# Hymba decode step on one core: mLSTM numerators issued head by head instead of in pairs of heads

## The reference

```python
    S = jnp.einsum('bhtd,bhsd->bhts', q, k) * D
    num = inter[..., None] * jnp.einsum('bhtd,bhde->bhte', q, C) + jnp.einsum('bhts,bhse->bhte', S, v)
    den = inter * jnp.einsum('bhtd,bhd->bht', q, n) + S.sum(axis=-1)
    h = num / jnp.maximum(jnp.abs(den), jnp.exp(-m_t))[..., None]
    C_new = decay[..., None, None] * C + jnp.einsum('bhs,bhsd,bhse->bhde', w, k, v)
```

## Time and profile before

| what | value |
|---|---|
| median of three runs | 2631.05 us |
| the profiled execution's own time | 2632.91 us |
| its span | 2631.1 us |
| TensorE matmul busy | 2475.9 us (94%) |
| VectorE busy | 1315.3 us (50%) |
| ScalarE busy | 879.6 us (33%) |
| chain that ended last, TensorE's share | 83% |
| mean granted TensorE clock | 0.96 |

### The profile page before, as it was taken

How to read it: one execution, slowest core, us unless ns; L and a number is a source line. 1 busy time by engine, 2 the same in 40 slices (tenths; PEclk the granted TensorE clock), 3 DMA queues, 4 the chain that set the end, 5 groups by cost and what they waited for, 6 DMA issues and landing times.

```text
span 2631.1 us, 32793 instructions
## 1 busy us (share of the span) xinstructions
PE 2475.9 (94%) x13299; PEld 2088.3 (79%) x13299; DVE 1315.3 (50%) x2562; ACT 879.6 (33%) x1544; POOL 51.5 (2%) x87
## 2 busy tenths in 40 slices
PE   6998999999998999999998999999996799999996
PEld 5886888887886888887886888888995669888885
DVE  4467444445467444445467444445265445444443
ACT  3343322233353322233344322233334123222221
POOL 2000000000000000000000000000021000000000
PEclk8999999999999999999999999999995599999998
DMA  5211223234311223334311233234211212222221
GB/s 181 81 49 49 88 93 95 93 112 157 89 49 49 85 91 97 96 104 160 87 53 50 80 96 97 90 111 160 76 49 39 21 59 81 81 72 81 80 81 56
DMA packets 180947, 224.85 MB, mean 85 GB/s; under 512 B 21003, under 2 KB 131636, under 8 KB 180780
## 3 DMA queue, kind: packets, MB, share of 16 engines
q1 hardware_dynamic: 164700, 190.34, 23.4%
q10 hardware_dynamic: 12000, 24.94, 2.8%
q0 software_dynamic: 4096, 7.47, 1.4%
HBM read 211.30 MB, written 12.60 MB: 85 GB/s over the span
## 4 chain that ended last, share of the span: by engine, by line
PE 83%; DVE 8%; DMA 3%; ACT 3%; issue 2%; ACTq 0%; POOL 0%; SPq 0%; DVEq 0%; POOLq 0%
PE ps L1752 25%; PE ps L1754 24%; PE ps L1753 24%; DMA w_raw<-in_w_in_dram 2%; PE ps L1829 2%; DVE w_lo L992 2%; PE ps L1809 1%; PE ps L1874 1%; PE ps L1847 1%; PE ps L1818 1%; ACT w_hi L588 1%; DVE a_lo L996 1%; DMA out_dram<-vm 1%; DVE x L996 1%; ACT PT L628 1%
## 5 line engine op out<-in xcount | busy, mean ns | idle before, releaser
L1752 PE MATMUL ps<-a_hi,w_hi 128*128 128x512 f32 (+2 forms) x1688 | 593.6, 352 | 31.0 <-DVE a_lo L996 14.1
L1754 PE MATMUL ps<-a_hi,w_lo 128*128 128x512 f32 (+2 forms) x1688 | 594.5, 352 | 0.0
L1753 PE MATMUL ps<-a_lo,w_hi 128*128 128x512 f32 (+2 forms) x1688 | 593.2, 351 | 0.0
L588 ACT ACTIVATE w_hi<-w_raw 128x1024 fp32r<-128x1024 f32 (+2 forms) x368 | 365.5, 1034 | 662.2 <-PE ps L1754 591.8
L992 DVE TENSOR_TENSOR w_lo<-w_raw,w_hi 128x1024 fp32r<-128x1024 f32 (+2 forms) x368 | 438.2, 1200 | 208.8 <-ACT w_hi L588 208.0
L1752 PE MATMUL ps<-w_hi,u_hi 128*128 128x512 f32 (+1 forms) x1088 | 431.1, 396 | 10.4 <-DVE x L996 10.4
L1754 PE MATMUL ps<-w_hi,u_lo 128*128 128x512 f32 (+1 forms) x1088 | 430.7, 396 | 0.0
L1753 PE MATMUL ps<-w_lo,u_hi 128*128 128x512 f32 (+1 forms) x1088 | 429.8, 395 | 0.0
L1752 PEld LDWEIGHTS ps<-a_hi,w_hi 128*128 128x128 f32 x1688 | 322.7, 191 | 76.3 <-issue 21.2
L1753 PEld LDWEIGHTS ps<-a_lo,w_hi 128*128 128x128 f32 x1688 | 321.0, 190 | 41.9
L1754 PEld LDWEIGHTS ps<-a_hi,w_lo 128*128 128x128 f32 x1688 | 320.9, 190 | 40.0
(11 more groups left out here) (299 smaller groups left out, 1964.7 us busy)
## 6 DMA issues: line engine op xcount, KB each, us to landing
w_raw<-in_w_up_dram SPq DMA_DIRECT2D x128, 512.0 KB, 3.6
w_raw<-in_w_down_dram SPq DMA_DIRECT2D x128, 512.0 KB, 3.5
w_raw<-in_w_out_dram SPq DMA_DIRECT2D x32, 512.0 KB, 3.9
w_raw<-in_w_in_dram SPq DMA_DIRECT2D x24, 580.0 KB, 3.9
w_raw<-in_w_in_dram SPq DMA_DIRECT2D x24, 512.0 KB, 3.7
x<-in_x_prompt_dram ACTq DMA_DIRECT2D x16, 512.0 KB, 6.4
w_raw<-in_w_in_dram SPq DMA_DIRECT2D x32, 256.0 KB, 3.1
wide<-in_x_prompt_dram ACTq DMA_DIRECT2D x12, 512.0 KB, 4.3
```

Of the source, the lines that this page charges most:

```text
L588: eng.activation(w_hi[b][:, k * n:(k + 1) * n], raw[p % RAW][:, 0:n], ACT.Copy).then_inc(w_high.sem, 1)
L1752: eng.matmul(out, lh, rh, start=(k == ks[0]), stop=False)
L1753: eng.matmul(out, lh, rl, start=False, stop=False)
L1754: ins = eng.matmul(out, ll, rh, start=False, stop=(k == last))
```

## The change

Only the order of the matmul calls in `numerators` changes. Before, the two heads of a pair i (one in each half of the partitions) came together: the two `ST` matmuls, then the two `qI` matmuls. After, each head's `ST` matmul is followed by its own `qI` matmul, for h = 0, 1, 2, 3. Operands, outputs, waits and the signal at the end are the same.

```diff
-                for i in range(2):
-                    out = [ps[2 + par][:, i * (DV + 1):(i + 1) * (DV + 1)] for par in range(2)]
-                    for par in range(2):
-                        eng.matmul(out[par], ST[:, 2 * i + par, :], vm[:, j, 2 * i + par, :], start=True, stop=False)
-                    for par in range(2):
-                        rs = slice(par * DK, (par + 1) * DK)
-                        ins = eng.matmul(out[par], qI[rs, i, :], Cst[rs, i, :], start=False, stop=True)
+                for h in range(HM):
+                    i, par = h // 2, h % 2
+                    rs = slice(par * DK, (par + 1) * DK)
+                    out = ps[2 + par][:, i * (DV + 1):(i + 1) * (DV + 1)]
+                    eng.matmul(out, ST[:, h, :], vm[:, j, h, :], start=True, stop=False)
+                    ins = eng.matmul(out, qI[rs, i, :], Cst[rs, i, :], start=False, stop=True)
                 ins.then_inc(n_out.sem, 1)
```

## The result

The changed kernel takes 2659.62 us, median of four runs (2657.57 to 2660.61), against 2631.98 us of the kernel before in four runs: 27.6 us more, ratio of the runs 1.010, 95% interval 1.0087 to 1.0113. The prediction had the direction; it had 2649.2 us, with 2641 to 2655 as the forecast and 2657 as the upper end of its range, and the time lies above both. The profiled execution took 2658.38 us.

What follows compares the result with a forecast made beforehand. It took TensorE, holding 83% of the span, as what counts except in its waits: 9.9 us in quarters 0 to 2 plus 8.2 in the last, 18.1 in all, on 2631.05 gave 2649.2 us; range 2641 to 2655, chance 0.78.

Steps and rivals of the forecast that it cites:

- The price of a group: TensorE groups in `numerators`: time is slots plus row-count changes; 1.2 us more a chunk at full clock, 2.05 at half.
- a slot: TensorE time of one record, or of two paired on both row halves: 0.11 us at full clock, 0.21 at half.
- a change: Switch between matmul operands of 128, 64 and 4 rows on TensorE: adds 0.20 us, 0.31 at half clock.
- What of it lies on the path: Loss left after waits: 3.3 us in each of quarters 0 to 2; the last quarter's section adds 8.2 us.
- the idle before chunk 1: TensorE's 0.20 us idle before `ST` of chunk 1, quarter 0; forecast gone, the wait swallowing 0.36 us.
- The clock falls inside quarters 0 to 2: Rival: longer short-matmul stretches lower the clock in every second of 12 chunks, adding 20 us, 2669; chance 0.06.
- signs of being wrong: A group of two clearly under 0.42 us, changed clock in chunk stretches, or idle behind chunk 3 shrinking over 1.1 us.
- the clock comes back: Rival: busier TensorE lifts the last quarter's clock from 0.50 to 1.00; 20 us faster, 2611; chance 0.03.
- The small version: Behind chunk 3, idle shrinks from 5.50 to 4.4 us and the clock stays up: up to 8 us saved, 2641.
- The 56 ns for a slot: Skill-based price of a 129-column slot, making the whole loss 15 us; set aside for the rows' 0.11 us.

Runs made afterwards that it cites:

- pairing lost: Kernel before, but both `qI` matmuls of a pair read the first half of the rows, so numerators differ; 2640.56 us, ratio 1.0031.
- one change less: Kernel before, with a chunk reordered: `ST` of heads 0 and 1, all four `qI`, `ST` of heads 2 and 3; 2627.23 us, ratio 0.9988.
- the filled halves: Changed kernel plus, beside each `qI` matmul, another on the idle half of the rows into unread columns; 2646.65 us, ratio 1.0071 against the kernel before.
- all rows in use: Changed kernel's head-by-head order, but `qI` and `Cst` run over all 128 rows, so numerators differ; 2627.73 us, ratio 0.9988 against the kernel before.

## Why the prediction was wrong

- The price of a group held. Blocks of 3.24 and 5.79 us were forecast as 3.3 and 5.8; a slot of 0.11 us and a change of 0.20 us were each seen by themselves (pairing lost: 0.64 for 0.42 us; one change less: 1.90 for 2.10 us).
- "What of it lies on the path" held: the idle before chunk 1 gone, 0.1 us left of chunk 3, 8.3 us in the last quarter for 8.2. With most of the falls gone by the filled halves, the whole was 18.4 us for a forecast 18.1. That it comes so close is partly luck: a fall and a faster stretch behind chunk 3, neither in the sum, are both in the 18.4 us, and the interval is 3 us to either side.
- The step that failed is a term that the sum put at nothing: the clock in the chunks of quarters 0 to 2, which it took to stay at 1.00. The rival "The clock falls inside quarters 0 to 2" got 0.06 and a price of 20 us. It is what happened: 24 us at half clock, at a price of some 9.2 us (changed kernel against the one with the halves filled), about half of the rival's. 2649.2 plus 9.2 is 2658.4; measured was 2659.6. A changed granted clock in chunk stretches was among the prediction's own signs of being wrong, and it is the one that came.
- The argument against it was a wrong comparison. Rows 10 show 5.5 us of short matmuls at clock 1.00, and I took from them that short matmuls keep the clock. Most of them (32 of 48 records) run over all 128 rows without a change between; the new blocks leave half the rows idle in every second group. A row that could have warned was used elsewhere: in rows 9 the clock stays at 0.50 with TensorE busy for 17.8 of 20 us, in blocks that are even paired. I read that as "it will not come back" alone. That row does not show whether the blocks or the short idle gaps before them keep the clock down; with all rows in use it came back in part at 85% busy.
- The case "the clock comes back" did not occur in the changed kernel; in the kernel with all rows in use it occurred in part (0.63).
- The small version, less half clock behind chunk 3 as the idle shrinks, is seen in quarters 0 and 2 of the changed kernel (6.8 to 3.4 us at half clock) and in all three quarters with the halves filled, so it is in the 27.6 and in the 18.4 us and does not explain the 9.2 between them. The shorter idle is not enough for it: with the changed order in chunk 3 alone the idle is 4.48 us and the clock behind it is 0.74 as before. What decides it stays open.
- The 56 ns for a slot, set beside the rows in the prediction, were not the right figure to compare: the Trainium skill, TensorE: Matmul & The Clock Gate, Back-to-back issue gap, gives N/2.4 + 2.5 for an isolated matmul and about 81 ns at 128 columns for a stream with weight loads. The 0.11 us of the rows lie above both, and the sum goes by the rows.

Not settled is why the clock fell after some chunks of this kind and not after others, and how the lost pairing and the added changes share in it: in the chunks of quarters 0 to 2, lost pairing alone gave 6.6 us at half clock, both together 24, the changes alone (halves filled) 3.4. Each of these is one profiled execution, and the times of the kernels with lost pairing and with chunks 0 to 2 alone spread over 10 us and more, so their falls may differ from run to run.

## What to carry to other kernels

Two matmuls on different halves of the rows should be issued next to each other, and matmuls of one row count kept together: here each record that loses its partner costs a slot (0.11 us at full clock) and each change of row count 0.20 us. Before trusting a sum of durations on TensorE, ask of the new stretch how much of the array works in it, and not only how busy the engine looks, and compare it with a stretch of the same kind in the trace at either clock. An engine that idles behind a block does not make the block free: ask which engine's chain ends the idle, and where that chain starts.

## What the runs showed of the hardware

- The granted clock fell to half while the profile showed TensorE busy without a gap (44.5 of 44.5 us, clock 0.92), and did so with idle halves of the array but hardly with filled ones at the same busy time (41.2 of 41.2 us, 1.00). The Trainium skill, TensorE: Matmul & The Clock Gate, Part 1, has the gate follow how busy the engine has been. The profile's busy time does not show that here: both stretches are busy throughout, and their clocks differ.
- More work was faster: with added `qI` matmuls beside each head's own, 27.6 us over before became 18.4.
- A pair on two halves starts within 0.01 us (196.65 and 196.66) and costs 0.42 us a group, no more than the half alone (0.41 or 0.42).
